# Hybrid decoder layer on one core: the first chunk of x arrives and is rounded in two parts

## The reference

```
h = x @ w_in                     # x: 512 tokens x 1024, w_in: 1024 x 3008
qa, ka, va, ga, iq, ik, iw, c_q, c_kv, k_rope, gb = split(h)
# branch A: indexer scores -> top 128 keys per query -> softmax attention over those keys
score = sum_h iw_h * relu(iq_h . ik) ; p = softmax over the top keys ; o_a = p @ va
# branch B: low-rank q and kv, rotary key, causal softmax attention
out = concat(o_a * silu(ga), o_b * silu(gb)) @ w_out
x   = layernorm(alpha * x + out)
```

## Time and profile before

| | |
|---|---|
| median of 3 runs | 286.03 us (285.81 to 286.28) |
| the profiled execution's own time | 285.56 us |
| its span in the profile | 283.8 us |
| PE busy | 274.0 us, 97% of the span |
| DVE busy | 235.6 us, 83% |
| POOL busy | 180.4 us, 64% |
| ACT busy | 149.9 us, 53% |
| DMA, mean rate over the span | 125 GB/s |

### The profile page before, as it was taken

One profiled execution on the slowest core, in us unless ns is written; L12 is line 12 of the kernel. 1 busy time (PEld: TensorE's weight loads), 2 busy tenths in 40 slices (PEclk: granted clock), 3 DMA queues, 4 the chain that ended last, 5 costly groups with the idle time before them and its releaser, 6 DMA issues.

```text
span 283.8 us, 5132 instructions
## 1 busy us (share of the span) xinstructions
PE 274.0 (97%) x1664; PEld 228.7 (81%) x1664; DVE 235.6 (83%) x541; ACT 149.9 (53%) x352; POOL 180.4 (64%) x196
## 2 busy tenths in 40 slices
PE   8999989999999999999999999999999999999990
PEld 8999967678888888888888888886778788888890
DVE  2899999989999999999984698678695967986375
ACT  5656534575433377215177696786765774552000
POOL 5998947323099999999935994885699932010012
PEclk9999999999999999999999999999999999999997
DMA  7986552222604297221238751917900000545022
GB/s 251 364 254 191 148 161 74 74 76 55 167 13 138 74 223 224 74 74 39 74 74 217 237 141 47 252 43 251 374 5 2 0 1 3 167 110 169 0 76 74
DMA packets 20874, 35.41 MB, mean 125 GB/s; under 512 B 6928, under 2 KB 9488, under 8 KB 20592
## 3 DMA queue, kind: packets, MB, share of 16 engines
q1 hardware_dynamic: 20272, 34.79, 41.3%
q10 hardware_dynamic: 576, 0.29, 0.4%
HBM read 26.69 MB, written 2.10 MB: 101 GB/s over the span
## 4 chain that ended last, share of the span: by engine, by line
PE 75%; DVE 17%; issue 2%; DMA 2%; SPq 1%; POOL 1%; ACT 1%; DVEq 0%; ACTq 0%; POOLq 0%
PE ps L1301 36%; PE ps L1624 16%; PE ps L1541 6%; PE ps L1502 5%; DVE score L1069 4%; PE ps L1562 3%; PE ps L1586 3%; PE ps L1484 2%; DVE x_lo L948 2%; DVE lat_tok L1046 2%; PE ps L1487 2%; DMA x_raw<-in_xT 2%; DVE trig_tmp L975 1%; DVE rope_tmp L990 1%; DVE idx_tok L993 1%
## 5 line engine op out<-in xcount | busy, mean ns | idle before, releaser
L596 POOL TENSOR_TENSOR w_lo<-w_raw,w_hi 128x512 fp32r<-128x512 f32 (+3 forms) x62 | 83.0, 1363 | 23.5 <-ACT w_hi L738 22.7
L738 ACT ACTIVATE w_hi<-w_raw 128x512 fp32r<-128x512 f32 (+3 forms) x62 | 35.9, 595 | 53.3 <-PE ps L1301 50.1
L849 ACT ACTIVATE probs<-probs,small 128x512 f32<-128x512 f32 (+3 forms) x64 | 35.7, 559 | 23.2 <-DVE small L1131 22.7
L1624 PE MATMUL ps<-wo_hi,oT 128*128 128x512 f32 (+1 forms) x144 | 45.4, 388 | 0.0
L1301 PE MATMUL ps<-w_hi,x_lo 128*128 128x512 f32 (+3 forms) x120 | 43.0, 362 | 0.0
L1301 PE MATMUL ps<-w_lo,x_hi 128*128 128x512 f32 (+3 forms) x120 | 42.9, 361 | 0.0
L1301 PE MATMUL ps<-x_hi,w_hi 128*128 128x512 f32 x96 | 38.0, 396 | 0.0
L1301 PE MATMUL ps<-x_hi,w_lo 128*128 128x512 f32 x96 | 37.4, 390 | 0.0
L1301 PE MATMUL ps<-x_lo,w_hi 128*128 128x512 f32 x96 | 37.4, 390 | 0.0
L1301 PE MATMUL ps<-w_hi,x_hi 128*128 128x512 f32 (+2 forms) x84 | 32.1, 382 | 0.0
L1624 PEld LDWEIGHTS ps<-wo_hi,oT 128*128 128x128 f32 x144 | 25.9, 189 | 5.2 <-issue 0.2
(11 more groups left out here) (191 smaller groups left out, 627.9 us busy)
## 6 DMA issues: line engine op xcount, KB each, us to landing
w_raw<-in_w_in SPq DMA_DIRECT2D x20, 512.0 KB, 3.7
kaT_swap<-kaT SPq DMA_DIRECT2D x8, 256.0 KB, 3.8
w_raw<-in_w_out SPq DMA_DIRECT2D x4, 512.0 KB, 4.9
wo_early<-in_w_out SPq DMA_DIRECT2D x4, 512.0 KB, 4.9
wo_raw_b<-in_w_out SPq DMA_DIRECT2D x4, 512.0 KB, 5.1
x_res<-in_x SPq DMA_DIRECT2D x4, 512.0 KB, 6.8
x_raw<-in_xT SPq DMA_DIRECT2D x3, 512.0 KB, 5.8
out_y<-y SPq DMA_DIRECT2D x6, 256.0 KB, 2.3
```

The lines of the kernel that those rows point to most:

```text
L596: pool.tensor_tensor(w_lo[:, s, 0:n], w_raw[:, s, 0:n], w_hi[:, s, 0:n], ALU.subtract).then_inc(w_lo_ready, 1)
L738: act.activation(dst, w_raw[:, s, 0:n], ACT.Copy).then_inc(w_hi_ready, 1)
L849: act.activation(probs[:, u % NPROBS, 0:N], probs[:, u % NPROBS, 0:N], ACT.Exp, bias=neg_max[:, u % 8:u % 8 + 1], scale=-1.0, accum_out=ro ...
L1624: ins = mm(out_ps(i, b), oT[i % 2][:, o, k, :], w[:, wcols], start=first, stop=final)
```

## The change

Chunk 0 of x is brought in by two transfers on the SP queue instead of one: first tokens 128 to 511 (three row tiles, 192 KB), then tokens 0 to 127 (64 KB, rows of 512 bytes) with a semaphore of its own. DVE rounds it in two instructions instead of one, each behind its own transfer. PE's first hi-hi products (indexer group, row tiles 1 to 3) wait for the first part only; the latents' products of chunk 0, and the low part of chunk 0 on DVE, wait for both.

```
             for q, (a, b) in enumerate(((0, 1), (1, 2), (2, 4), (4, 6), (6, 8))):
-                sp.dma_start(x_raw[:, a:b, :], xT_v[:, a:b, :]).then_inc(x_loaded[q], 16)
+                if q == 0:
+                    sp.dma_start(x_raw[:, 0, P:SEQ], xT_v[:, 0, P:SEQ]).then_inc(x_loaded[0], 16)
+                    sp.dma_start(x_raw[:, 0, 0:P], xT_v[:, 0, 0:P]).then_inc(first_tile_loaded, 16)
+                else:
+                    sp.dma_start(x_raw[:, a:b, :], xT_v[:, a:b, :]).then_inc(x_loaded[q], 16)
...
-                dve.wait_ge(x_hi_ready if k > 0 else x0_hi_ready, max(k, 1))
+                dve.wait_ge(x_hi_ready if k > 0 else x0_hi_ready, k if k > 0 else 2)
                 V.tensor_tensor(x_lo[:, k, :], x_raw[:, k, :], x_hi[:, k, :], ALU.subtract).then_inc(x_lo_ready, 1)
...
             dve.wait_ge(x_loaded[0], 16)
-            V.tensor_copy(x_hi[:, 0, :], x_raw[:, 0, :]).then_inc(x0_hi_ready, 1)
+            V.tensor_copy(x_hi[:, 0, P:SEQ], x_raw[:, 0, P:SEQ]).then_inc(x0_hi_ready, 1)
+            dve.wait_ge(first_tile_loaded, 16)
+            V.tensor_copy(x_hi[:, 0, 0:P], x_raw[:, 0, 0:P]).then_inc(x0_hi_ready, 1)
...
                         g, k = FRONT[step]
-                        pe.wait_ge(x_hi_ready if k > 0 else x0_hi_ready, max(k, 1))
+                        pe.wait_ge(x_hi_ready if k > 0 else x0_hi_ready, k if k > 0 else 1 if g == G_IDX else 2)
```

More of the change, by code:

```diff
@@ L264, in build @@
         first_loaded, second_loaded = sem("first_loaded"), sem("second_loaded")
+        first_tile_loaded = sem("first_tile_loaded")
         w_loaded = [sem(f"w_loaded{i}") for i in range(RPAIR)]
```

## The result

| | before | after |
|---|---|---|
| median of 22 runs each, us | 285.77 | 286.31 |
| lowest to highest, us | 285.25 to 286.34 | 285.83 to 286.76 |
| profiled execution, us | 285.56 | 286.36 |
| its span, us | 283.8 | 284.6 |

The ratio is 1.002 with an interval of 1.0013 to 1.0027. The change costs 0.54 us (0.37 to 0.77 us); the profiled executions lie 0.80 us apart.

A forecast was written before the change was run, and what follows sets the result against it. The prediction took the DVE and POOL turns from weight chunk 4's landing to `ik_st`, where PE waits, as the bound. Its terms, 0 + 0 + 0 + 0.08, gave about +0.1 us, or 286.1 us, range 285.5 to 286.8 us.

The forecast's parts named there:

- The bound: DVE and POOL take turns from weight chunk 4's landing to `ik_st`, where PE waits 1.11 us; delays there move the end.
- First term: PE's first hi-hi products: chunk 0 of x is ready first, so its earlier arrival removes nothing; 0.
- Second term: DVE's extra rounding instruction and wait: up to 0.43 us more, covered by idle time ahead of later low parts; 0.
- Third term: SP's extra transfer: loads from weight chunk 1 issued 0.45 us later, hidden by time in the queue; 0 where it holds.
- Fourth term: DMA packets: 128 more, 8 on each of 16 engines at 10 ns, delay weight chunk 4 by 0.08 us.
- (a): Late stream: issue delay not hidden and small packets cost a mean one; weight chunk 4 0.80 us later, 286.8 us; chance 0.16.
- (c): A turn won: a DVE instruction between 8.78 and 37.74 us runs in a POOL gap, gaining 0.65 us, 285.4 us; chance 0.14.
- (b): A lost turn: DVE's first low part starts behind POOL's first subtraction at 4.80 us, +0.43 us, 286.5 us; chance 0.14.
- (d): PE's earlier first product reaches the end through weights landing 0.17 us earlier, 285.9 us; chance 0.06.
- The tell-tale: ACT's row for weight chunk 4 starting at 9.5 us or later would show the cover by the queue was wrong.

The follow-up runs named there:

- round_only: Kernel before with chunk 0 of x in one load but rounded in two instructions, with PE's waits of the change: 285.79 against 285.65 us, ratio 1.0001.
- late_more: Kernel before with SP waiting behind its first load for POOL's fifth constant, other SP loads about 1.5 us later, no packet more: 287.56 against 286.06 us.
- load_only: Kernel before with chunk 0 of x in two loads as in the change, but rounded once behind both: 286.24 against 285.65 us, ratio 1.0016.
- change_w1_on_act: The change with weight chunk 1 issued by ACT, so SP issues the rest no later than before: 286.15 against 286.01 us for the kernel before.
- second_on_act: The change with the second part of chunk 0 issued by ACT behind weight chunk 0: 286.01 against 285.65 us for the kernel before, ratio 1.0011.
- late_issue: Kernel before with SP waiting behind its first load for a POOL constant, later loads issued 0.35 us later, no packet added: 286.06 against 286.01 us.
- rows_split: Kernel before with chunk 0 of x loaded in two halves of partitions, whole 2 KB rows, one rounding: 286.9 against 285.65 us, ratio 1.004.
- w12_on_act: Kernel before with weight chunks 1 and 2 issued by ACT and the position loads moved behind on SP: 286.28 us against 286.01, ratio 1.0014.
- angles_early: Kernel before with DVE's first two angle instructions ahead of the low part of chunk 2 of x: 285.98 against 286.06 us, ratio 0.9994.

## Why the prediction was wrong in its sum

The measured +0.54 us lies in the stated range and just under the 0.57 us that the prediction could tell from no change, but that it does is luck: the interval reaches to 0.77 us, the sum was +0.1 us, and the forecast of no change rested on a cover that wasn't there.

- **The bound** was read rightly: DVE and POOL start from the landing of the pair and set the end, as the table shows. That the whole of it would show at `ik_st` was not: DVE's instructions alternated ahead of it, and the lateness came out at the ReLU, whose wait of 0.4 us was the second of the two.
- **First term, 0:** right. The first product did not start sooner (4.85 us). The tenths won by weight chunk 0 were not even kept: chunk 1 came later, PE stood 0.51 us and was 0.96 us late from 7.24 us on. The idle time ahead of `ik_st` took that, and with it nearly all of the 1.11 us that the prediction counted on.
- **Second term, 0:** right by `round_only`, +0.0 us (-0.2 to +0.3 us).
- **Third term, 0:** this is the step that failed. "Since the bytes ahead are the same, a later issue only shortens the time in the queue" would have kept the time of landing and cut the time from issue to landing from 4.98 us to about 4.5 us. Here are both from the views of DMA issues (KB each, us from issue to landing), first before, then after, for chunks 2 and 3 of x and for weight chunk 5:

```profile
x_raw<-in_xT SPq DMA_DIRECT2D x1, 512.0 KB, 5.0
...
w_raw<-in_w_in SPq DMA_DIRECT2D x1, 228.0 KB, 5.0
```

```profile
x_raw<-in_xT SPq DMA_DIRECT2D x1, 512.0 KB, 5.8
...
w_raw<-in_w_in SPq DMA_DIRECT2D x1, 228.0 KB, 5.8
```

It rose to 5.8 us, and to 6.0 us in `late_more`; in `load_only`, with the same later issue, it was 5.2 us, and in no profile of a later issue did it fall. The argument took the 1.03 us beyond an empty-engine landing for a store of work ahead of the load. But the engines are busy for only 0.79 of the time from 2 to 3 us even before the change, and after it for 0.74 from 4.0 to 4.5 us; in `late_more` they are not full until 5 us. What isn't moved then is moved later. `late_more` is the clearest proof: 1.5 us of later issue cost 1.5 us (1.0 to 2.1 us), although the cover for the pair was put at 2.2 us and more. That figure was also misread: it took the landing of weight chunk 5 for that of chunk 4. Chunk 5, with 228 KB, took 5.0 us, which leaves 1.7 us beyond the 3.28 us of chunk 0 of x, and these were no cover either.

The Trainium skill ("DMA: Bandwidth & Descriptors", section "Anatomy of one DMA — SWDGE (gpsimd) path") counts a fixed time and a time for the bytes of each transfer; that each landing follows its own issue is what the prediction drew from it, and so worked out 286.5 us. The page fits this to transfers that GpSimd issues, while those here are issued by SP and ACT. In direction it was the better guide: +0.5 us against the measured +0.54 us, and 1.5 us for 1.5 us in `late_more`. In size of one transfer it stays off: 5.0 to 6.0 us from issue to landing here.

- **Fourth term, 0.08 us:** not separable. The trace counts 144 packets more, 128 for the rows and 16 below 512 bytes that come with one more transfer. The added packets alone cost 0.0 us (`change_w1_on_act`, -0.2 to +0.3 us) to 0.3 us (`second_on_act`, 0.0 to 0.6 us), 0.35 us of later issue alone 0.0 to 0.34 us at most, both together 0.46 us (`load_only`) and 0.54 us (the change). From 3 to 4 us the trace leans to a higher price. Packets, MB and share of SP's queue, after and then `late_issue`:

```profile
q1 hardware_dynamic: 265, 0.25, 85.3%
```

```profile
q1 hardware_dynamic: 168, 0.27, 75.6%
```

By the prediction's line (38 ns for a KB, 10 ns for a packet) the second would be 0.27 MB x 38 + 168 x 10 ns = 11.9 us, 75% of 16 engines, as measured; the first 12.2 us, 76%, but it is 85.3%. The 1.5 us more over at most 128 small packets are an estimate of 12 ns for each on top of the 10 ns. The bytes are rounded to 0.01 MB, or 0.4 us, so this is a hint; `load_only` gives one of the same sign (242 packets, 0.23 MB, 78.2% where the line has 70%). How the loss divides between issue and packets stays open.

- **The rivals.** (a) is what happened in mechanism: the stream was late, and DVE and POOL with it. The place was another, since the wait at L1394 didn't grow to 1.9 us but vanished, and that a small packet costs as much as a mean one isn't shown. That its 0.80 us is also the difference of the profiled executions is chance: the landing moved by 1.3 us in the profile, and 0.25 us of the 1.17 us at the marker were given back by the turn of rival (c), which was real but did not win; the net was 0.92 us on DVE. By the medians it was 0.54 us. (b), the lost turn at 4.8 us, didn't come: the second part was there by 4.22 us. (d) was taken up by waits, as said against it.
- **The tell-tale** named for a wrong cover, an ACT row for the pair at 9.5 us or later, appeared at 10.40 us. I had read the queue only from 6 us on, where it is full. The share of 0.79 from 2 to 3 us, just where the extra issue pushes the others back, would have been a warning, though no proof: from 3 us on the engines are full in the trace of before.

## What to carry to other kernels

The time by which a landing exceeds that on empty engines was no slack for its issue. In this stream at the start of a program each extra transfer on the issuing queue delays the issue of all that stand behind it; 1.0 and 1.5 us of that cost 1.1 and 1.5 us (`rows_split`, not a clean one, and `late_more`), while the loss from 0.35 us was too small to tell from nothing (`late_issue`). Gaps in the DMA engines' work before they are full are the likely reason, not a shown one, since `late_issue` landed late with full engines. Before counting on a queue, read the engines' share microsecond by microsecond from the first issue on, and test the cover by a wait on the issuing queue. Ask also whether the consumers have idle time to win: here POOL had 0.26 us, so earlier loads had little to win.

## What the hardware showed beyond that

- The time from issue to landing of the same 512 KB was 5.0 us before and 5.2 us in `round_only`, and with a later issue 5.2 us (`load_only`), 5.8 us (the change, `late_issue`) and 6.0 us (`late_more`), though the bytes ahead of it were the same. Issued 0.94 us earlier, in `w12_on_act`, it took 5.9 us. Landings also leave the order of issue: after the change weight chunk 4, issued behind chunks 2 and 3 of x at 4.02 us, landed 4.8 us later at 8.8 us, before their 9.36 us. Why a load's slowest part lags so is open.
- Splitting the load by partitions cost SP more than splitting it by columns: 1.22 us for two halves against 0.87 us for two parts of the tokens (0.74 to 1.61 us), and the next issue took 0.59 us.
- Beside POOL's subtractions of about 1.2 us, DVE got one or two short instructions into a gap, and the second costs 0.16 to 0.18 us instead of 1.3 us. What decides it is open. The change alternates and the kernel before doesn't, but `angles_early`, which reaches these instructions only 0.07 us earlier than the kernel before (32.65 against 32.72 us), alternates too:

```profile
33.85 0.18 DVE L989 TENSOR_TENSOR rope_tmp<-idx_tok,trig 128x32 f32<-128x32 f32 x1
```
